# Turning the feed-forward product by a transposing DMA instead of TensorE, in a two-block fp32 kernel

## The reference

```
h = rms_norm(x, g_ffn_pre)
gate, up = split(h @ w_gate_up)               # w_gate_up: 2048 x (2 * 5632)
x = x + rms_norm((silu(gate) * up) @ w_down, g_ffn_post)   # w_down: 5632 x 2048
```

## Time and profile before

| | |
|---|---|
| median of 3 runs | 2174.43 us (2173.81 to 2174.7) |
| the profiled execution | 2174.46 us, span 2172.6 us |
| TensorE, VectorE, ScalarE busy | 99%, 70%, 51% of the span |
| DMA in the feed-forward part | 0.90 of the engines' time, 300 GB/s (706 to 760 us) |
| granted TensorE clock | full in all of it |

### The profile page before, as it was taken

The page is one execution under the profiler, slowest core; times in us unless marked ns, Lnnn a source line. Parts: engine busy times, 40 slices in busy tenths (PEclk is TensorE's granted clock), DMA queues, the critical chain, the costliest instruction groups (busy, mean ns, idle before and its releaser), DMA issues.

```text
span 2172.6 us, 27740 instructions
## 1 busy us (share of the span) xinstructions
PE 2161.0 (99%) x10891; PEld 1792.7 (83%) x10891; DVE 1517.0 (70%) x1948; ACT 1106.4 (51%) x1485; POOL 46.6 (2%) x66
## 2 busy tenths in 40 slices
PE   9999999999999999999999999999999999999999
PEld 7888887888888888888888888887898887888887
DVE  6675479778867777777777778767455568556566
ACT  6676466444446444444433444566456455555542
POOL 0000000100000000000000000000000000000000
PEclk9999999999999999999999999999999999999999
DMA  9544655598886899998999898574565574655573
GB/s 333 165 146 146 194 177 173 167 394 293 278 305 214 299 304 303 309 309 299 305 299 313 301 312 294 190 235 135 158 187 151 165 246 129 182 170 164 155 241 118
DMA packets 242131, 502.87 MB, mean 231 GB/s; under 512 B 16960, under 2 KB 21296, under 8 KB 240848
## 3 DMA queue, kind: packets, MB, share of 16 engines
q1 hardware_dynamic: 238704, 486.20, 68.9%
q0 software_dynamic: 3296, 14.88, 2.0%
HBM read 498.89 MB, written 2.12 MB: 231 GB/s over the span
## 4 chain that ended last, share of the span: by engine, by line
PE 94%; DVE 2%; DMA 1%; ACT 1%; issue 1%; SPq 0%; POOL 0%; DVEq 0%; ACTq 0%
PE bank L972 91%; PE bank L975 3%; ACT arena L1403 1%; DMA raw<-in_w_in 1%; DMA arena<-in_w_in 1%; DMA raw<-in_w_ple_gate 0%; DVE wl L2021 0%; DVE hl L2021 0%; ACT wh L1403 0%; DVE arena L2024 0%; ACT ah L1403 0%; DVE arena L2028 0%; SPq L767 0%; DVE arena L2029 0%; DVE al L2021 0%
## 5 line engine op out<-in xcount | busy, mean ns | idle before, releaser
L1403 ACT ACTIVATE wh<-raw 128x1024 fp32r<-128x1024 f32 (+1 forms) x496 | 519.2, 1049 | 644.1 <-PE bank L972 591.5
L2021 DVE TENSOR_TENSOR wl<-raw,wh 128x1024 fp32r<-128x1024 f32 (+1 forms) x496 | 599.1, 1210 | 343.5 <-ACT wh L1403 341.8
L972 PE MATMUL bank<-wh,hh 128*128 128x512 f32 (+1 forms) x1568 | 615.6, 394 | 1.9 <-DVE wl L2021 0.8
L972 PE MATMUL bank<-wh,hl 128*128 128x512 f32 (+1 forms) x1568 | 605.0, 387 | 0.3 <-DVE hl L2021 0.2
L972 PE MATMUL bank<-wl,hh 128*128 128x512 f32 (+1 forms) x1568 | 604.0, 386 | 0.0
L972 PE MATMUL bank<-wh,ah 128*128 128x512 f32 x1104 | 433.6, 394 | 1.1 <-ACT arena L1403 0.7
L972 PE MATMUL bank<-wh,al 128*128 128x512 f32 x1104 | 429.2, 390 | 0.0
L972 PE MATMUL bank<-wl,ah 128*128 128x512 f32 x1104 | 428.6, 389 | 0.0
L972 PEld LDWEIGHTS bank<-wh,hh 128*128 128x128 f32 x1568 | 294.3, 188 | 61.0 <-DVE wl L2021 2.4
L972 PEld LDWEIGHTS bank<-wh,hl 128*128 128x128 f32 x1568 | 294.1, 188 | 60.7 <-DVE hl L2021 1.1
L972 PEld LDWEIGHTS bank<-wl,hh 128*128 128x128 f32 x1568 | 294.7, 188 | 55.7
(11 more groups left out here) (142 smaller groups left out, 1486.3 us busy)
## 6 DMA issues: line engine op xcount, KB each, us to landing
raw<-in_w_in SPq DMA_DIRECT2D x245, 512.0 KB, 3.7
arena<-in_w_ada SPq DMA_DIRECT2D x148, 384.0 KB, 4.8
arena<-in_w_gate_up SPq DMA_DIRECT2D x97, 512.0 KB, 4.4
raw<-in_w_ada SPq DMA_DIRECT2D x108, 384.0 KB, 4.8
raw<-in_w_out SPq DMA_DIRECT2D x80, 512.0 KB, 4.9
raw<-in_w_gate_up SPq DMA_DIRECT2D x79, 512.0 KB, 4.4
raw<-in_w_down SPq DMA_DIRECT2D x45, 512.0 KB, 5.1
arena<-in_w_down SPq DMA_DIRECT2D x43, 512.0 KB, 5.2
```

The source lines that it names most:

```text
L972: return i.matmul(o, l, x, start=start, stop=stop, skip_group_check=False)
L1403: return i.activation(o, x, fn, scale=scale, **k)
L2021: return i.tensor_tensor(o, a, b, op)
```

## The change

For the blocks 0 to 9 (block 10 stays as it was):

- TensorE's generator `up` returns without transposes.
- ScalarE, in slot t0+1, waits for the product and copies it as 16-bit numbers into `HALVES`: first the lower 16 bits of every word, then the upper ones (two instructions, each 1024 elements a partition). It waits for its own copies and, from block 1 on, for VectorE's use of the last result. Then it issues `dma_start_transpose` from `HALVES` to `TURN`: 128 partitions x 2048 16-bit elements, 512 KB, which is 16 blocks of 128x128.
- In slot t0+3 ScalarE waits for the landing and for VectorE's last subtraction, and copies one plane back into every other 16 bits of `TURNED`. VectorE waits likewise (for the landing and ScalarE's last rounding) and copies the other plane, ahead of its unit's subtraction.
- In slot t0+4 ScalarE waits for both planes and for the `down` units that used the operand, and rounds all four tile rows of `TURNED` into `hh` in one instruction. VectorE waits for that and subtracts into `hl`, in one instruction too.
- VectorE's eviction of `up` waits for ScalarE's copies of the block two before, where it waited for TensorE's transposes.
- The three buffers take the arena's places 40, 44 and 48. The feed-forward part's window keeps 52 and 60, so the ring has six places where it had nine.

```diff
@@ -9,6 +9,7 @@
 F32 = mybir.dt.float32
 F32R = mybir.dt.float32r
 I32 = mybir.dt.int32
+U16 = mybir.dt.uint16
 ALU = mybir.AluOpType
 ACTF = mybir.ActivationFunctionType
 AX = mybir.AxisListType
@@ -261,7 +262,7 @@
 WINDOWS = [((16, 20, 24, 28), -1, 23, "start"),
            ((8, 12, 16, 20, 24, 28), slot("gates", 6) + 1, slot("wo", 0) - 2, "hgrn"),
            ((8, 12), slot("wo", 0) - 1, slot("gate", 0) - 1, "hgrn"),
-           ((40, 44, 48, 52, 60), slot("wo", 0) + 6, slot("down", 11) + 3, "merged")]
+           ((52, 60), slot("wo", 0) + 6, slot("down", 11) + 3, "merged")]
 
 
 @dataclass
@@ -628,6 +629,8 @@
         ADA = [kb(80, 3), kb(83, 3)]
         XR, YR, GR = two(64, 16), two(16, 16), kb(32, 8)
         G_, U_ = [two(0, 4), two(4, 4)], [two(8, 4), two(12, 4)]
+        TURNED, TURN = kb(40, 4), kb(44, 4).bitcast(U16)
+        HALVES = kb(48, 4).bitcast(U16)
         E_, PN = two(40, 16), kb(56, 2).rearrange("p (k t) -> p k t", k=2)
         CS_ = [kb(o, 3)[:, 0:2 * 258].rearrange("p (k n) -> p k n", k=2) for o in (61, 48)]
         CC_ = [kb(o, 1) for o in (60, 52)]
@@ -690,6 +693,16 @@
         def mla_stat(z, j, k):
             o = 166 + 12 * z + 6 * (j % 2) + 2 * k
             return ST[:, o:o + 2]
+
+        def last_pair(c):
+            z, p0 = next((z, a) for z, (a, b) in enumerate(FPARTS) if a <= c < b)
+            return f"H3{z}", 2 * (c - p0) + 1
+
+        def flat(half):
+            return TURN.rearrange("p (m z k t) -> p m z k t", m=2, z=2, k=4)[:, :, half, :, :]
+
+        def word(half):
+            return TURNED.bitcast(U16).rearrange("p (k m t z) -> p m k t z", k=4, m=2, z=2)[:, :, :, :, half]
 
         def pair_of(ph, p):
             hi, lo = OPND[ph[0]]
@@ -1214,6 +1227,8 @@
                 yield
                 yield
                 z = next(z for z, (a, b) in enumerate(FPARTS) if a <= c < b)
+                if c < 10:
+                    return
                 e.wait_ge(*S.v_ev.at(INDEX["up", c]))
                 for p in range(2):
                     t_pair(f"H3{z}", 2 * (c - FPARTS[z][0]) + p, U_[c % 2][:, :, p * 256:(p + 1) * 256])
@@ -1699,10 +1714,34 @@
 
             def up(c):
                 yield
-                yield
-                z = next(z for z, (a, b) in enumerate(FPARTS) if a <= c < b)
+                z, (p0, p1) = next((z, ab) for z, ab in enumerate(FPARTS) if ab[0] <= c < ab[1])
+                if c < 10:
+                    e.wait_ge(*S.v_ev.at(INDEX["up", c]))
+                    nat = U_[c % 2].bitcast(U16).rearrange("p m (n z) -> p m n z", z=2)
+                    for half in range(2):
+                        x = copy(HALVES.rearrange("p (m z n) -> p m z n", m=2, z=2)[:, :, half, :], nat[:, :, :, half])
+                    x.then_inc(*S.a_halves.up(c))
+                    e.wait_ge(*S.a_halves.at(c))
+                    if c:
+                        e.wait_ge(*S.v_word.at(c - 1))
+                    i.dma_start_transpose(TURN.rearrange("p (j t) -> p j t", t=P), HALVES).then_inc(*S.d_turn.dma(c))
+                    yield
+                    yield
+                    e.wait_ge(*S.d_turn.at(c))
+                    if c:
+                        e.wait_ge(*S.v_op.at(*last_pair(c - 1)))
+                    copy(word(0), flat(0)).then_inc(*S.a_word.up(c))
+                    yield
+                    q = 2 * (c - p0)
+                    e.wait_ge(*S.v_word.at(c))
+                    e.wait_ge(*S.a_word.at(c))
+                    e.wait_ge(*S.p_unit.at(before(f"H3{z}", q)))
+                    copy(OPND["H"][0][:, 2 * q:2 * q + 4, :].rearrange("p k t -> p (k t)"), TURNED).then_inc(*S.a_op.up(f"H3{z}", q + 1))
+                    S.a_op.name(f"H3{z}", q)
+                    return
+                yield
                 for p in range(2):
-                    split(f"H3{z}", 2 * (c - FPARTS[z][0]) + p)
+                    split(f"H3{z}", 2 * (c - p0) + p)
                     yield
 
             def down(n):
@@ -2441,14 +2480,26 @@
                 e.wait_ge(*S.a_ev.at(INDEX["gate", c]))
                 part = next(z for z, (a, b) in enumerate(FPARTS) if a <= c < b)
                 if c > 1:
-                    k = c - 2
-                    old = next(z for z, (a, b) in enumerate(FPARTS) if a <= k < b)
-                    e.wait_ge(*S.p_op.at(f"H3{old}", 2 * (k - FPARTS[old][0]) + 1))
+                    e.wait_ge(*S.a_halves.at(c - 2))
                 for m in range(2):
                     x = stt(U_[c % 2][:, m, :], acc(z, m), R1[:, m:m + 1], G_[c % 2][:, m, :], ALU.mult, ALU.mult)
                 x.then_inc(*S.v_ev.up(z))
                 yield
                 yield
+                if c < 10:
+                    yield
+                    e.wait_ge(*S.d_turn.at(c))
+                    if c:
+                        e.wait_ge(*S.a_op.at(*last_pair(c - 1)))
+                    i.tensor_copy(word(1), flat(1)).then_inc(*S.v_word.up(c))
+                    yield
+                    ph, q = last_pair(c)
+                    q -= 1
+                    e.wait_ge(*S.a_op.at(ph, q + 1))
+                    hi, lo = (t[:, 2 * q:2 * q + 4, :].rearrange("p k t -> p (k t)") for t in OPND["H"])
+                    tt(lo, TURNED, hi.bitcast(F32), ALU.subtract).then_inc(*S.v_op.up(ph, q + 1))
+                    S.v_op.name(ph, q)
+                    return
                 for p in range(2):
                     split(f"H3{part}", 2 * (c - FPARTS[part][0]) + p)
                     yield
```

## The result

The changed kernel takes 2215.8 us (median of 6 runs, 2207 to 2225), the kernel before 2174.7 beside it: a ratio of 1.0188, 95% interval 1.017 to 1.0205. It is **41 us slower**. I had forecast 2165, with a range up to 2204. The profiled execution is the slowest of the six: 2225.2 us, span 2223.4, 50.8 more than before.

The account below looks back on a forecast made before the run. It took TensorE, busy 99% of the span, to bound the kernel: 2174.4 us less 9.6 for removed transposes, nothing for the rest, plus 0.2 for two blocks' thin margin, gave 2165.0; own range 2163.5 to 2170, 8-in-10 range 2163 to 2204.

Parts of the forecast that it names:

- The landing: Step pricing the 512 KB transposing DMA from weight-load rows: 5.2 us, bounds 3.8 and 10.5, as the DMA engines had room.
- L: Assumed landing time of the transposing DMA, 5.2 us; stalls of L - 6.9 in eight blocks, L - 5.4 in two.
- A: Rival: late landing keeps ScalarE and VectorE standing in line behind it; 2204 us at a 10.5 us landing; chance 0.14.
- E0: Time origin of each block's schedule: end of an `up` block's last unit, in slot t0; DMA issue expected 6.0 us later.
- the rest that I had as the tightest (t0+4): VectorE's rest for slot t0+4, expected ready at 17.0 us and due at 18.7, spare 1.7 us.
- TensorE's 9.6: Gain from removing twenty transpose groups between `up` and `down` in ten blocks, 0.48 us each: 9.6 us.
- The copies on ScalarE and VectorE: Added copies, rounding and subtraction: 3.1 us a block more on ScalarE, 1.1 on VectorE; no rate problem.
- Six places alone: Feed-forward ring cut from nine landing places to six: a place returns every 9.3 us, needs 7.1 to 8.5; cost nothing.
- The line of times: Per-block schedule of ScalarE and VectorE around the landing: spare times 2.4, 1.7 and 2.3 us, no stall; 0.2 in two blocks.
- Rival B: The issue holds ScalarE's queue, taken as 0.4 us; if held for the whole 5.2 us, 2184 us; chance 0.07.
- Rival C: Six landing places are too few in the feed-forward part; with steady 6.5 us landings, 2201 us; chance 0.06.
- Rival A2: The DMA's sixteen 128x128 blocks go one after another; landing 32 us, 2419 us, or 20.9 and 2308; chance 0.06.

Follow-up runs that it names:

- e11: Separate small program, not the kernel: 512 KB transposing DMAs beside load streams with pieces of 512 bytes to 4 KB; median landings 10.5, 12.5, 16.6 and 24.0 us.
- e10: Changed kernel with nine landing places and the transposing DMA issued from SP's queue ahead of slot t0+6's loads, waits at t0+3, ten blocks: 2167.9 us, ratio 0.9964.
- e12: Changed kernel, six places, ten blocks, with the transposing DMA issued from SP's queue ahead of the loads for slot t0+5: 2173.2 us, ratio 0.9993.
- e5: Changed kernel with all nine landing places kept, buffers moved into the gate's and product's own, same slots and waits: 2215.4 us, ratio 1.018.
- e3: Changed kernel without its transposing DMA and the waits for it, so the product is not turned: 2166.2 us, ratio 0.9955.
- e6: Changed kernel with nine places, wait moved to t0+7, eight blocks (3 and 7 turned by TensorE): 2167.9 us, ratio 0.9964.
- e1: Kernel before with six landing places instead of nine in the feed-forward part, TensorE still turning every block: 2175.0 us, ratio 0.9997.
- e7: Changed kernel with nine places, wait moved to t0+4, eight blocks (3 and 7 turned by TensorE): 2181.7 us, ratio 1.0026.
- e9: Changed kernel with nine places, wait moved to t0+5, eight blocks (3 and 7 turned by TensorE): 2168.1 us, ratio 0.9965.
- e2: Kernel before with ten 512 KB transposing DMAs added on ScalarE's queue into a buffer nobody reads, nine places: 2175.9 us, ratio 0.9999.
- e4: Changed kernel, six places, wait moved from t0+3 to t0+7, blocks 3 and 7 turned by TensorE: 2172.5 us, ratio 0.9986.
- e8: Separate small program, not the kernel: transposing DMAs of 32 to 512 KB alone, then 512 KB beside weight loads; 512 KB landed in 4.3 us alone, 16.7 beside.

## Why the prediction was wrong

**What failed is the step "The landing".** It took L = 5.2 us and, as its upper bound, 10.5. The median was 11.9 and the longest 16.9. The step's reason was that the DMA engines move 300 GB/s here and 393 elsewhere and so "have room". Room for bytes is the wrong measure: e11 shows that beside a full stream a second queue of small packets waits for turns, and in the change its own packets and those of the loads took longer too, while the bytes moved fell to half (159 GB/s for 307, in the first block). A load of the same size was the wrong row for it: it has 256 packets of 2 KB, this has 2080. My L would have been near in the loads' queue (medians of 4.6 in e10 and 6.5 in e12), which is where the loads whose rows I took it from were issued. The prediction never asked which queue.

**The rival that came about is A**, ranked at 0.14. Its price of 2204 at L = 10.5 becomes 2218 at L = 11.9 by its own formula (8 x 5.0 + 2 x 6.5 - 9.6 = 43); 2216 was measured. That agreement is partly luck. With the landing of each block the formula gives 53 us of stalls in the change and 44 in e5, and TensorE was idle for 42 and 32. In the first block of the change it gives 4.8 us, and 3.1 were seen: the half went back on VectorE in 0.74 us instead of 1.22, the issue stood at E0 + 5.7 instead of 6.0, and the rest that I had as the tightest (t0+4) kept nobody waiting, with TensorE at its lower clock by then. That clock, not in my sum, makes up for the rest.

**What held.** TensorE's 9.6: 9.8 in e3, 7.6 for eight blocks in e6. The copies on ScalarE and VectorE: no cost in rate (e3). Six places alone: no cost (e1). The line of times, with a wait at t0+3 and a due time some 5.5 us after it: e7 and e9 moved as it says, a slot at a time. But it was too strict by about 1 us a block.

**Sizes.** Halves 1.99 us for both (priced 2.1); one half put back 1.35 on ScalarE (1.06) and 0.74 on VectorE (1.22). The issue holds ScalarE's queue for 1.3 to 5.4 us, median 4.4, where I had 0.4. Rival B's hold is thus real, and the row of SP's load that I put against it was the wrong one. By itself it cost nothing in e2, e6 and e9. In the change, in block 3, where ScalarE was already late for want of weights, a hold of 5.4 us is followed by 1.2 us of idle time (the row at 865.96), ahead of the long gap. Whether a hold of 4 us would cost something beside a landing of 5 stays open: e10 took both away at once.

**Rival C** has a true core: six places are enough for the loads alone, and seem too few beside the transposing DMA (e4 against e6: 4.6 us, with TensorE's idle time before `wl` and ScalarE's before weights). e12 lies 5.3 us over e10, but there the slot of the issue differs too. **Rival A2 is out:** e8's 512 KB alone take 4.3 us, twice what 32 KB take, not sixteen times. One block of 128x128 is 32 KB, and it landed here in 2.2 us, most of it fixed cost, since fifteen more add 2.1. The Trainium skill has 1309 ns for it (VectorE: DVE Perf Modes, The three transpose paths), less than was measured here; sixteen times that figure takes it for a rate, which it isn't. What I put against A2, "spread over all queues at once", holds for the 16 engines; in the profile each issue's packets lie in one queue, q1 or q10.

**The rule against the rows.** In the change such a DMA took 11.9 us, beside 3.8 for a load of the size before. The Trainium skill's rule that the two are equally fast (Advanced Engine Details and Errata, X-Bar Transpose) nearly holds alone and in the loads' own queue, 4.3 and 4.6 us, and fails by a factor of three in a queue of its own beside the loads. The Trainium skill also says (DMA: Bandwidth & Descriptors, Issuing engines are not separate DMA queues) that DMAs from several engines run on the same 16 DMA engines and interleave. e11's packets agree, one for one, and it is this interleaving that I should have priced.

**What stays open.** Turns of one packet each are counted beside e11's full stream. In the kernel the counts are others, and what makes the packets themselves slower there is not known. Of the 18 us put down to the clock, 13 are counted in TensorE's timeline and the rest is a remainder.

## What to carry to other kernels

Before a DMA is put on a second queue, look at its packets and not at its bytes, and time it beside the stream that it will meet: the same 512 KB took 4.3 us alone, 4.6 in the loads' queue, 11.9 in a second queue in this kernel and up to 24 beside a full stream of large packets. Where an in-order engine waits for a transfer, its slot is worth more than any count of busy time: with nine places, two slots later in eight blocks, or the loads' own queue in ten, turned 41 us of loss into 7.5 of gain. And a long gap on TensorE costs more than its length, since the matmuls behind it can run at the lower clock for a while.

## What the runs showed of the hardware

- A transposing DMA of 512 KB has 2080 packets. It lands in 4.3 us alone, 3.1 for 256 KB, 2.4 for 128 KB and 2.2 for 32 KB (e8).
- Beside a full stream of loads in another queue it takes 10.5 us (pieces of 512 bytes) to 24.0 (4 KB), with one packet of the loads for each of its own (e11). In the loads' queue it takes 4.6 with nine places and 6.5 with six (e10, e12).
- In a second queue in the change it takes 11.9, with 395 packets of the loads to its 2080 in the first block; its packets take 45 ns in the mean there, 18 in e11.
- It holds its issuing queue: 1.3 to 5.4 us on ScalarE in the change, 2.0 to 3.7 on SP with nine places and 3.7 to 5.0 with six, against 0.37 for a load.
- A 16-bit copy of 1024 elements with a stride on one side took 0.74 us on VectorE, and a float32 subtraction of that size 1.22; on ScalarE the strided write took 1.35 and the strided read 0.99.
- After a gap of 10.6 us TensorE's matmuls were 0.43 us apart for thirteen intervals, then 0.23 again; after e7's gaps, the longest of 1.7 us, they were not.
